# A decoder layer with block-sparse attention: later q tiles, the pooling branch and part of the merge interleaved with the attention steps

## The reference

```python
h = rms_norm(x, norm_mix)
q, k, v, u, g_a, g_p = split(h @ w_in)      # widths 512, 512, 512, 512, 1024, 1024
q = partial_rope(rms_norm(q, q_norm), pos)  # 8 heads of 64; rotary on the first 16 dims
k = partial_rope(rms_norm(k, k_norm), pos)
# attention: each query sees its own block of 256 keys (causal) and the 3 of the
# fully past blocks with the largest q . mean(k of the block)
o_attn = moba_attention(q, k, v)
# trailing means over 2, 4, 8, 16 tokens, one per group of 128 channels, minus the token,
# then a 128x128 product per group and a scale per channel
o_pool = multiscale_pool(u, w_pool_grp, pool_scale)
m = sigmoid(g_a) * (o_attn @ w_up_attn) + sigmoid(g_p) * (o_pool @ w_up_pool)
x = x + m @ w_out
x = x + square(relu(rms_norm(x, norm_mlp) @ w_ff1)) @ w_ff2
```

## Time and profile before

| | |
|---|---|
| median of 4 runs | 1045.6 us (1035.97 to 1080.64) |
| the profiled execution, its own time | 1035.97 us |
| its span, on the slowest core | 1034.9 us |
| spans of the eight cores | 1022.4 to 1034.9 us |
| TensorE busy in it | 946.0 us (91%) |
| VectorE, ScalarE, POOL busy | 476.5 us (46%), 403.0 us (39%), 103.3 us (10%) |

### The profile page before, as it was taken

The page is one execution under the profiler, slowest core; times in us unless marked ns, Lnnn a source line. Parts: engine busy times, 40 slices in busy tenths (PEclk is TensorE's granted clock), DMA queues, the critical chain, the costliest instruction groups (busy, mean ns, idle before and its releaser), DMA issues.

```text
span 1034.9 us, 17973 instructions; the slowest of 8 cores (1022.4 to 1034.9 us)
## 1 busy us (share of the span) xinstructions
PE 946.0 (91%) x5944; PEld 493.6 (48%) x6028; DVE 476.5 (46%) x876; ACT 403.0 (39%) x755; POOL 103.3 (10%) x172
## 2 busy tenths in 40 slices
PE   0498999698999979999989999999999999999997
PEld 0254544576887534444445444444444444444443
DVE  0286666645444334444456544443444444444443
ACT  1377576798999412222212353303110211111110
POOL 0154310420000111211010100000000000000000
PEclk9899999799999999999999999999999999999999
DMA  8963030300000483963076090235005500001123
GB/s 200 203 121 103 1 92 1 32 2 3 3 2 3 61 82 32 251 86 30 2 157 109 8 156 1 32 50 82 1 1 82 82 1 1 1 1 41 62 82 142
DMA packets 57688, 62.11 MB, mean 60 GB/s; under 512 B 27584, under 2 KB 50240, under 8 KB 57472
## 3 DMA queue, kind: packets, MB, share of 16 engines
q0 software_dynamic: 49040, 30.18, 23.0%
q1 hardware_dynamic: 8560, 30.79, 8.5%
HBM read 80.65 MB, written 8.39 MB: 86 GB/s over the span
## 4 chain that ended last, share of the span: by engine, by line
PE 84%; DMA 7%; DVE 3%; issue 3%; ACT 2%; SPq 1%; POOL 0%; DVEq 0%; ACTq 0%; POOLq 0%
PE bank L1135 21%; PE bank L1109 21%; PE bank L434 9%; PE bank L763 7%; PE bank L944 5%; PE bank L1011 5%; PE bank L940 4%; DMA raw<-w_in 4%; PE bank L796 3%; DMA raw<-x 3%; PE bank L948 2%; PE bank L952 2%; PE bank L1044 1%; ACT raw L769 1%; PE bank L511 1%
## 5 line engine op out<-in xcount | busy, mean ns | idle before, releaser
L1135 PE MATMUL bank<-raw 128*128 128x512 bf16 x1004 | 221.9, 379 | 1.1
L1109 PE MATMUL bank<-raw 128*128 128x512 bf16 x1003 | 221.9, 379 | 1.1
L1116 ACT ACTIVATE raw<-bank 128x512 f32<-128x512 f32 x128 | 76.4, 597 | 318.1 <-PE bank L1109 316.4
L1135 PEld LDWEIGHTS bank<-raw 128*128 128x128 bf16 x1024 | 100.3, 98 | 120.7
L1109 PEld LDWEIGHTS bank<-raw 128*128 128x128 bf16 x1024 | 100.0, 98 | 120.7
L1118 DVE SCALAR_TENSOR_TENSOR raw<-bank,raw 128x512 bf16<-128x512 f32 x128 | 88.5, 692 | 143.8 <-ACT raw L1116 139.1
L769 ACT ACTIVATE raw<-bank 128x512 bf16<-128x512 f32 x288 | 146.1, 645 | 6.9 <-PE bank L796 5.9
L1141 DVE SCALAR_TENSOR_TENSOR raw<-bank,raw 128x512 f32<-128x512 f32 x128 | 96.1, 751 | 113.0 <-PE bank L1135 112.7
L434 PE MATMUL bank<-raw 128*128 128x512 bf16 x498 | 117.5, 387 | 14.6 <-DMA raw<-w_in 7.9
L763 PE MATMUL bank<-raw 128*128 128x256 bf16 x576 | 109.3, 278 | 7.7 <-ACT raw L532 3.5
L434 PEld LDWEIGHTS bank<-raw 128*128 128x128 bf16 x512 | 48.9, 99 | 71.3 <-issue 19.3
(11 more groups left out here) (103 smaller groups left out, 805.7 us busy)
## 6 DMA issues: line engine op xcount, KB each, us to landing
raw<-x SPq DMA_DIRECT2D x32, 512.0 KB, 12.6
raw<-w_ff POOLq DMA_DIRECT2D x16, 1024.0 KB, 12.9
out<-raw SPq DMA_DIRECT2D x16, 512.0 KB, 2.7
raw<-w_in POOLq DMA_DIRECT2D x4, 1024.0 KB, 23.5
raw<-w_in POOLq DMA_DIRECT2D x16, 256.0 KB, 6.7
raw<-c_zero SPq DMA_DIRECT2D x8, 256.0 KB, 3.4
raw<-raw SPq DMA_DIRECT2D x1, 2048.0 KB, 9.0
raw<-w_out POOLq DMA_DIRECT2D x2, 1024.0 KB, 15.1
```

The source lines that it names most:

```text
L1109: t.group("pe", [lambda e, c=c, j=j, bk=bk: e.matmul(bank_f(bk), lhsT=ffw1[s][:, c, j * 128:(j + 1) * 128], rhs=hT[:, c, tg * 512:(tg + 1) ...
L1116: t.op("act", lambda e, bk=bk, si_=si_: e.activation(out=sqz[si_], in_=bank_f(bk), func=AF.Square), reads=hb[bk], writes=[b_sqz[si_]])
L1135: t.group("pe", [lambda e, j=j, bk=bk, hf=hf, i=i: e.matmul(bank_f(bk), lhsT=a1T[ab][:, j, i * 128:(i + 1) * 128], rhs=ffw2[s][:, j, hf * ...
```

## The change

The program is rewritten; the reference's result is the same. What it does:

- Buffers get a first and a last stage, and `plan` places them; a buffer waits at its first use only for those whose bytes it takes (`Region`), not for a snapshot of everything. The tracker also leaves out waits that follow from earlier ones.
- Constants come in bfloat16, so that the identity, a triangular mask and the pooling matrices are plain DMAs on SP. x tile 0 is SP's first DMA; POOL's queue starts with K and V weights in halves; SP waits for V's second half before x tiles 4 to 7, POOL before the q weights and a memset of the q buffer `qz`.
- The projections have 36 jobs: all of K and V, and q tiles 0 to 3. x's inverse root is a multiply-add and a power on POOL (`rsqrt_pool`) in place of ScalarE and VectorE. The copy to hT goes from ScalarE to VectorE, V's from VectorE to ScalarE; rotation works in PSUM ahead of the head scaling, on VectorE alone; K is written in two halves into kA and kB, whose other halves are filled by eight DMAs of 256 KB.
- Attention has 144 steps, one a pair of heads and of key tiles: four score matmuls, one exponential of 1024 columns (768 on diagonals, where a second half is left out and the mask is added by a matmul of the identity with the triangle), and one step later eight matmuls with v (six on diagonals) into one bank. Normalising is done for each pair of heads.
- Between a step's scores and the last step's value products stand "fill" units, by a credit that is spread evenly over the steps: q tiles 4 to 15 (24 steps ahead of use, their roots on POOL), their ranking and bias rows (now sent by eight small DMAs on SP per tile), u, the pooling products, and the pool gate and pool up products of column blocks 0 and 1 (`NFB = 2`), kept as `mp0`, `mp1`.
- Sigmoid(z) becomes (1 + tanh(z/2)) / 2, with the half taken in the out projection's addition.
- The merge leaves out what attention has done; slices are loaded two blocks ahead, behind the last use of their slot; x tiles 0 to 11 are loaded two a block behind a wait of SP for VectorE. The gain vector takes the bytes of `mp0`. Tiles go in the order 0 to 15 in the out projection and token groups 0 to 3 in feed-forward, whose instructions are else the same.

The plan puts the merge's weight slices (`wga`, `wua`, `wgp`, `wup`) on the bytes of kB, `wu` on those of buffers that the projections use to their end, and the feed-forward weights on kA, kB, mT and the slices.

The core of the diff:

```diff
+def plan(wanted, base, end):
+    placed = []
+    where = {}
+    for name, size, a, b in sorted(wanted, key=lambda w: (-(w[3] - w[2] + 1) * w[1], w[0])):
+        size = (size + 31) // 32 * 32
+        busy = sorted((o, o + s) for o, s, pa, pb in placed if pa <= b and a <= pb)
+        at = base
+        for lo, hi in busy:
+            if at + size <= lo:
+                break
+            at = max(at, hi)
+        assert at + size <= end, ("no room", name, size, at, end)
+        placed.append((at, size, a, b))
+        where[name] = at
+    return where
...
-        def small_setup_rest():
-            t.wait_written("pool", b_xslot[7])
-            t.dma("pool", wqkvu[CG_Q], w_in_v[:, :, CG_Q * 512:(CG_Q + 1) * 512], writes=[b_wqkvu[CG_Q]])
-            t.dma("pool", wqkvu[CG_U], w_in_v[:, :, CG_U * 512:(CG_U + 1) * 512], writes=[b_wqkvu[CG_U]])
...
-        t.wait_written("pool", b_xslot[3])
-        t.dma("pool", wqkvu[CG_V], w_in_v[:, :, CG_V * 512:(CG_V + 1) * 512], writes=[b_wqkvu[CG_V]])
...
+        load_x(0)
+        load_w("wk", 1, 0)
+        load_w("wk", 1, 1)
+        load_w("wv", 2, 0)
+        load_w("wv", 2, 1)
+        t.dma("sp", A["gmix"], gmix_bc_d, writes=[b_gmix])
+        t.dma("sp", ident, c_ident_d, writes=[b_ident])
...
+        def rsqrt_pool(dst, src, b_dst, b_src, n, scale):
+            t.op("pool", lambda e: e.tensor_scalar(out=dst, in0=src, scalar1=scale, scalar2=EPS,
+                                                   op0=ALU.mult, op1=ALU.add),
+                 reads=[b_src], writes=[b_dst])
+            t.op("pool", lambda e: e.tensor_tensor(out=dst, in0=dst, in1=A["mhalf"][:, 0:n], op=ALU.pow),
+                 reads=[b_dst, b_mh], writes=[b_dst])
...
+        def in_rstd(tt):
+            rsqrt_pool(A["rstd1"][:, tt:tt + 1], A["ss1"][:, tt:tt + 1], b_rstd1[tt], b_ss1[tt], 1, 1.0 / D)
...
+        def head_stat(i, bank):
+            sq3 = A["sq%d" % i].rearrange("p (h d) -> p h d", h=H)
+            t.op("dve", lambda e: e.tensor_reduce(out=A["sta%d" % i], in_=sq3, axis=AX.X, op=ALU.add),
+                 reads=[b_sq[i]], writes=[b_sta[i]])
+            if in_stage[0]:
+                root_act(A["stb%d" % i], A["sta%d" % i], b_stb[i], b_sta[i], 1.0 / DH)
+            else:
+                rsqrt_pool(A["stb%d" % i], A["sta%d" % i], b_stb[i], b_sta[i], 8, 1.0 / DH)
...
+        for tt in range(13):
+            jobs += [("k", tt), ("v", tt)]
+        jobs += [("k", 13), ("q", 0), ("q", 1), ("k", 14), ("k", 15), ("q", 2), ("q", 3),
+                 ("v", 13), ("v", 14), ("v", 15)]
+        first_use = {}
+        for ji, (_, tt) in enumerate(jobs):
+            first_use.setdefault(tt, ji)
+        for tt in range(NT):
+            s0 = first_use[tt]
+            at(max(s0 - 6, -1), in_sq, tt)
+            at(max(s0 - 5, -1), in_rstd, tt)
+            at(max(s0 - 4, -1), in_mul, tt)
+            at(max(s0 - 2, -1), in_tr, tt)
+            if tt >= 8:
...
+        def zero_qz():
+            t.op("pool", lambda e: e.memset(A["qz"], 0.0), writes=[b for i in range(3) for j in range(2) for b in [b_qz[i][j]] + b_qzb[i][j]])
+
+        load_x(2)
+        load_x(3)
+        run(-1)
+        rope_gain("k", 32)
+        t.wait_written("sp", b_w["wv"][1])
+        for tt in range(4, 8):
+            load_x(tt)
+        t.wait_written("pool", b_w["wv"][1])
+        load_w("wq", 0, 0)
+        load_w("wq", 0, 1)
+        rope_gain("q", 0)
...
+        load_w("wu", 3, 0)
+        load_w("wu", 3, 1)
+        t.dma("pool", A["wgrp"], w_grp_d.rearrange("g c d -> c g d"), writes=[b_wgrp])
+        for fc in range(NFB):
+            t.dma("pool", A["bwg%d" % fc], w_in_v[:, :, 3072 + fc * 128: 3072 + (fc + 1) * 128], writes=[b_bwg[fc]])
+            t.dma("pool", A["bwu%d" % fc], w_up_v[:, :, fc * 128:(fc + 1) * 128], writes=[b_bwu[fc]])
+
...
+        def qk(i):
+            qb, pr, kp = steps[i]
+            sb0 = (i % 2) * 2
+            diag = kp == qb
+            for a in range(2):
+                h = 2 * pr + a
+                kx, bkx = (A["kA"], b_kA) if a == 0 else (A["kB"], b_kB)
+                fns = []
+                for j in range(2):
+                    kt = 2 * kp + j
+                    q0 = 128 if diag and j == 1 else 0
+                    fns.append(lambda e, kt=kt, j=j, q0=q0, kx=kx, h=h, a=a: e.matmul(
+                        bank_f(sb0 + a)[:, j * 256:j * 256 + 256 - q0], lhsT=kx[:, pr, kt * 128:(kt + 1) * 128],
+                        rhs=A["qz"][:, qb % 3, h, q0:256], start=True, stop=not diag, skip_group_check=True))
+                    if diag:
+                        fns.append(lambda e, j=j, a=a: e.matmul(
+                            bank_f(sb0 + a)[:, j * 256:j * 256 + 128], lhsT=ident, rhs=A["tri"],
+                            start=False, stop=True, skip_group_check=True))
+                t.group("pe", fns, reads=[bkx[2 * kp], bkx[2 * kp + 1], b_kfill[a], b_ident, b_tri] + b_qz[qb % 3] +
+                        [b_qzb[qb % 3][j][h] for j in range(2)],
+                        writes=[bk[sb0 + a]])
+            n = 384 if diag else 512
+            pt = A["pt%d" % (i % 3)]
+            s2 = bank_f(sb0, 2).rearrange("p (a c) -> p a c", a=2)
+            t.op("act", lambda e: e.activation(out=pt[:, :, 0:n], in_=s2[:, :, 0:n], func=AF.Exp, scale=0.125),
...
+        def pv(i):
+            qb, pr, kp = steps[i]
+            g = (qb * 4 + pr) % 3
+            bank = 4
+            diag = kp == qb
+            pt = A["pt%d" % (i % 3)]
+            fns = []
+            first = kp == 0
+            for a in range(2):
+                for j in range(2):
...
+                            bank_f(bank)[:, col:col + 65], lhsT=pt[:, a, c0:c0 + 128],
+                            rhs=A["v"][:, kt, 2 * pr + a, :], start=st, stop=True, skip_group_check=True))
+                        first = False
+            t.group("pe", fns, reads=[b_pt[i % 3], b_v[2 * kp], b_v[2 * kp + 1], b_vones], writes=[bk[bank]])
...
+        def o_norm(qb, pr):
+            g = (qb * 4 + pr) % 3
+            acc = bank_f(4)[:, 0:260].rearrange("p (l a d) -> p l a d", l=2, a=2)
+            rd = A["rden%d" % g]
+            hold("o", g)
+            t.op("dve", lambda e: e.reciprocal(out=rd.rearrange("p (l a) -> p l a", l=2), in_=acc[:, :, :, 64]),
+                 reads=[bk[4]], writes=[b_rden[g]])
+            t.op("dve", lambda e: e.tensor_tensor(
+                out=A["otok%d" % g].rearrange("p l (a d) -> p l a d", a=2), in0=acc[:, :, :, 0:64],
+                in1=rd.rearrange("p (l a) -> p l a", l=2).unsqueeze(3).to_broadcast([128, 2, 2, 64]), op=ALU.mult),
+                reads=[bk[4], b_rden[g]], writes=[b_otok[g]])
+
+        free_banks = [5, 6, 7]
...
+        def q_job(tt):
+            i = nrm_i[0] % 2
+            nrm_i[0] += 1
+
+            def posts(s, bank):
+                at(s + 1, head_sq, i, bank)
+                at(s + 1, head_stat, i, bank)
+                at(s + 2, head_rope, "q", i, tt, bank)
+                at(s + 3, head_mul, i, bank)
+                at(s + 3, release, bank)
+                at(s + 4, lambda: urgent.append(q_tr_job(i, tt)))
+            return Job([(853, lambda b: proj("wq", tt, b, 0, 4)), (853, lambda b: proj("wq", tt, b, 4, 8))], posts)
...
+                at(s + 1, lambda: t.op("act", lambda e: e.activation(
+                    out=A["tp%d" % i], in_=bank_f(bank), func=AF.Tanh, scale=0.5),
+                    reads=[bk[bank]], writes=[b_tp[i]]))
+                at(s + 1, release, bank)
+            return Job([(853, lambda b: mm(b, 0, 4)), (853, lambda b: mm(b, 4, 8))], posts), i
...
+                def evac():
+                    t.op("dve", lambda e: e.tensor_copy(out=A["bT%d" % i2], in_=bank_b(bank)[0:64, 0:128]),
+                         reads=[bk[bank]], writes=[b_bT[i2]])
+                    for h in range(H):
+                        lo = 64 if h % 2 == 0 else 0
+                        t.dma("sp", A["qz"][lo:lo + 8, qb % 3, h, c0:c0 + 128], A["bT%d" % i2][h * 8:(h + 1) * 8, :],
+                              reads=[b_bT[i2]], writes=[b_qzb[qb % 3][tt % 2][h]])
...
+        done_q = set(range(NQ0))
+        fill = []
+        for tg in range(4):
+            for tt in range(tg * 4, tg * 4 + 4):
+                fill.append(("u", tt))
+                if tt > 0:
+                    fill.append(("band", tt - 1))
+            if tg > 0:
+                fill += [("y", tg - 1, g) for g in range(4)]
+                fill += [("B", fc, tg - 1) for fc in range(NFB)]
+        fill.append(("band", 15))
+        fill += [("y", 3, g) for g in range(4)]
+        fill += [("B", fc, 3) for fc in range(NFB)]
+        q_at = {}
+        for tt in range(NQ0, NT):
+            q_at[tt] = max(0, first_step[tt // 2] - 24 + 5 * (tt % 2))
+        cost = {"u": 1706, "band": 430, "y": 213, "B": 2559}
+        total = sum(cost[f[0]] for f in fill) + 12 * 1950 + 8 * 300 + 32 * 110
+        QUOTA = total / (NS - 6)
...
```

(24 more changed lines are left out.)

1697 lines of the change are left out of this document (772 added, 925 removed).

## The result

The changed kernel takes 1014.6 us (median of all its runs; the kernel before 1038.6 in the same series). In some runs of either kernel the cores of one die are slower at a lower granted clock; without these it takes 1014.3, the ratio is 0.977 with a 95% interval of 0.973 to 0.982, and all times further down leave them out too. So it is faster, by about 2%.

What follows compares the result with a forecast made beforehand. TensorE's work, 913 us, was taken as the bulk, with about 122 us idle or slow clock to win. Stages ending at 120, 322, 473, 538 and 980, a 5.06 tail and 1.1 beyond the span gave 987 us; range 965 to 1020.

Steps and rivals of the forecast that it cites:

- Work on TensorE: All stages: matmul work totals 914 us against 913 before, so nothing is saved; attention's share is 188 us.
- The start: Projections: V weights land at 35 us (32 to 39), stalls are 12, and the stage ends at 120, against 181.4.
- the wait for tile 3: Projections: TensorE waits 4 us (bounds 0 and 9) for x tile 3, held behind POOL's queue with the qz memset.
- Merge: Merge's start: TensorE waits 5 us (3 to 9) for the first slices, 1 more for the clock, beside 145 of work.
- Tanh: Attention on ScalarE: Tanh brings no table reloads, so nothing was added; the rival with reloads gave 1007 us, chance 0.05.
- Roots on POOL: Projections and attention: POOL's power takes at most 1.135 us in the usual case and is covered by two jobs or steps.
- The rival in which a dear power makes the kernel slower: POOL's power holds up VectorE: from 3.3 us each it eats the 49 us gain, 1057 us at 4.1; chance 0.05.
- Attention's own stalls: Attention: waits for normalising, q copies and bias rows beside TensorE's work total 14 us, bounds 4 and 40.
- The prices on ScalarE: Attention: exponentials 0.92 and 0.71 us, copies, Squares and Tanhs of 512 columns 0.507; ScalarE has 160 us of work.
- A granted clock of 1.00: Attention: between 120 and 322 us the granted clock would be 1.00, with TensorE not waiting in most steps.
- Prices taken where nothing waits: TensorE's matmul prices: 0.216 us for 512 columns, 0.11 for 256, 0.056 for 128, 0.03 for 65.
- The first rival: Attention: ScalarE or handshakes pace it, another 0.2 us in each of 144 steps; 1016 us (1002 to 1030), chance 0.16.

Runs made afterwards that it cites:

- e11: On e5's kernel, the first gate and up slices of the merge get bytes of their own and load at attention's start; 1000.1 us, ratio 0.966.
- e3: Changed kernel with POOL's power left out for the 12 q tiles of attention; 1014.6 us, attention 230.2 us.
- e4: Changed kernel with the exponentials of the second head of each pair left out; 1009.4 us, attention 221.8 us.
- e5: Changed kernel with value products two steps behind their scores instead of one; 1005.8 us, ratio 0.972.
- e18: Changed kernel with only attention's q copies moved from ScalarE to VectorE, value products still one step behind; 1006.2 us, ratio 0.972.
- e1: Changed kernel with each later instruction of attention's fill chains emitted further behind the one that feeds it; 1017.2 us, attention 230.3 us.
- e9: On e5's kernel, fill chains get longer distances on both sides; 1013.4 us, attention 227.9 us.
- e13: On e11's kernel, each fill bank is handed to the next job one step later; 1003.8 us, attention 224.1 us.
- e16: On e11's kernel, e13's later hand-over, q copies on VectorE and fill units of two matmuls together; 1004.9 us, attention 225.1 us.

## Why the prediction was right in five stages and wrong in one

- *Work on TensorE.* Right outside attention. Nothing is saved, and the matmul prices give the stages: feed-forward 441.1 for 442, out projection 64.7 for 65. In attention they are short, as said below.
- *The start.* Right: V's first matmul at 34.73, forecast 35. The memset of qz took 5.26 us, forecast 6; the stage ended at 121.6, forecast 120. The sum behind it is in part luck: the wait for tile 3 was 1.39 us, not 4, and the stage's idle time was 86.86 - 78.50 = 8.4 us where 12 of stalls were taken, with a busy time of 78.5 where the work was 73.
- *Merge.* Right: a wait of 4.46 us for w_in, forecast 5, and 151.4 us in all, forecast 151. e11 shows that it was the transfer.
- *Tanh.* Right: one ACT_TABLE_LOAD in attention (1.283 us). The Trainium skill, "ScalarE: Activation LUTs" § Table sets, has both functions in one set; the trace agrees.
- *Roots on POOL.* Right in effect, wrong in the price: 1.639 us where the upper value was 1.135. e3 shows that it is covered. The rival in which a dear power makes the kernel slower needed 3.3 us.
- *Attention's own stalls.* This step failed: "Bounds 4 and 40; I take 14, near the lower as TensorE has 1.30 us a step to hide 0.92". The trace has 42 (and 230.1 us of attention, where the prediction called itself wrong above 230). The terms it named came out near its 14: normalising 6.5, the q copies 9.4, the bias rows nothing. What it had no term for, by that comparison of means, is the hand-over between TensorE and ScalarE in every step. Two things were wrong in it.
  - *The prices on ScalarE.* Exponentials were 1.023 and 0.811 us, not 0.92 and 0.71; copies and Tanhs of 512 columns 0.598, not 0.507. The forecast took the spacing of back-to-back exponentials and added a slope; here they stand mostly alone (41.8 us of idle time ahead of them), and each holds ScalarE for its whole duration. ScalarE had 175.3 us of work, not 160: of 202 us that leaves 0.19 us a step to spare, (202 - 175) / 144, and not 0.30. What this error alone cost no run shows; e4 took 52 us off ScalarE and won 7.7 by the medians. The Trainium skill, "ScalarE: Activation LUTs" § What ACT_TABLE_LOAD costs, gives 186 ns and 0.833 ns a column for one activation with immediate operands; an estimate by it is 1.04 for 1024 columns, and the trace's 1.023 agrees.
  - *An average stood for 144 steps.* Nearly as much work on two engines that hand over to each other every step is no cover when they may be only one step apart. What a step with much fill lets ScalarE idle, a step without fill doesn't get back: on core 3 of the changed kernel, whose records are complete, ten of the thirteen waits of a value product for an exponential stand where the step and the one before it hold at most 0.57 us of fill together (at 0.216 us for 512 columns; the mean of two steps is 1.2), and only 21 of 143 places hold so little. An eleventh is the last value product, with no fill left. e5 changes no work, only the distance, and wins 9.7 us; e18 takes two copies of 0.68 us out of ScalarE's queue, 12 times, and wins 9.4; both win 15.6.
- *Its other parts.* Normalising was sized right (6.5 of 3 to 10). The q copies had been given "up to 0.5 us, 24 times", that is up to 12, without a figure of their own in the 14; they were worth 9.4 with one step of distance and 5.2 with two (218.0 to 212.8). No wait of TensorE in attention ended with a DMA, so the bias rows' transfers cost nothing, of 0 to 5 a block.
- *A granted clock of 1.00.* It was 0.97 in the stage, 0.85 to 0.93 in parts of it, which is at most 7 of the 42 us, reached if TensorE had worked throughout the slow stretches. The windows are 12.41, 16.00 and 50.00 us long: 12.41 x 0.08 + 16.00 x 0.15 + 50.00 x 0.07 = 6.9.

```profile
121.59:134.00 12.41, 8.60 (x77) 5.57 (x77) 5.64 (x20) 7.51 (x11) 3.70 (x4) 0.92 1.19 130
134.00:150.00 16.00, 12.78 (x147) 9.60 (x148) 6.21 (x21) 12.37 (x17) 1.83 (x2) 0.85 0.02 3
150.00:200.00 50.00, 43.44 (x527) 30.58 (x533) 21.62 (x67) 37.38 (x46) 7.33 (x8) 1.00 0.01 3
200.00:250.00 50.00, 41.58 (x487) 29.34 (x491) 20.43 (x57) 35.84 (x42) 4.57 (x6) 0.93 0.01 2
250.00:351.70 101.70, 94.68 (x1180) 68.72 (x1195) 39.95 (x95) 82.16 (x95) 6.84 (x8) 1.00 0.01 2
```

The three stretches below 1.00 have the largest shares of idle time (31, 20 and 17%; the other two 13 and 7%). Here waits and a lower clock come together; which brings which no run shows.

- *Prices taken where nothing waits.* In e11 seven cores of eight have a granted clock of 1.00 in attention, and TensorE is busy 218.0 - 21.4 = 196.6 us for the 188 of work. So 8.6 us of attention are there neither idle time nor clock. A matmul's record lasts longer than its price where TensorE then stops (0.22 us for the 128 columns at 171.53 above, priced at 0.056); that this is all of the 8.6 us is argued, not shown.

This nearly closes the account. By the medians attention is 228.4 - 202 = 26 us longer than the forecast; the two repairs win 15.6 of them, clock included, and 8.6 are busy time beyond the prices, which leaves about 2.

The first rival, ScalarE or the handshakes pacing attention at 0.2 us a step more, has the size: 28 us over 144 steps are 0.19, and its time was 1016. Of its two causes the runs bear out the handshakes (e5, e18) and not ScalarE's pace (e4), and its 0.2 us was a size taken, so the near hit is in part luck. The argument against it, 0.30 us a step to spare, rested on the mis-sized prices and on the mean.

Open: after both repairs attention still has 213.5 - 188 = 25 us beside the work, 15.7 of it idle. Normalising, banks and VectorE's order each end some of it; spacing (e1, e9) and later release (e13, e16) made attention longer, and no run made it shorter. Two accumulation banks, or a fourth bank for fill, weren't tried.

## What to carry to other kernels

When work is moved under a loop in which two engines hand over to each other every iteration, compare them iteration by iteration and ask how many iterations apart they may be; 0.19 us to spare in the mean was none here. Price an instruction by its whole duration in the rows where it will stand alone, not by the spacing of a back-to-back run, and count every short copy that stands ahead of the one the loop waits for. Waits of 0.3 to 2 us that name many different releasers weren't mended one by one here (e1, e9, e13); a longer distance of the loop's main hand-over (e5) and less work in the queue ahead of it (e18) were what helped.

## What the runs showed of the hardware that was not expected

- A power on POOL costs 0.747 us for 128x1 and 1.639 us for 128x8 (16 and 12 of them in the changed kernel), while the multiply-add beside it took 0.473 us for 128x1 and 0.221 us for 128x8. If the two powers differ by their columns alone, that is (1.639 - 0.747) / 7 = 0.13 us a column, an estimate; they stand in different stages, and the multiply-add goes the other way. The Trainium skill, "GPSIMD Engine Reference" § Engine selection, has adds, multiplies and maxima of two inputs at about 2x VectorE's time; it names no power, and no run here has one on VectorE.
- A copy of half the partitions wasn't cheaper on ScalarE: 0.682 us for 64x512 from bfloat16 with a scale per partition, 0.598 us for 128x512 from float32 without. No run tells the three differences apart.
- A memset of 6144 bfloat16 columns on POOL took 5.257 us.
